# Two heads at a time on the two halves of the matrix array, in a two-block transformer kernel

## The reference, cut to what matters

```python
def _stick_breaking(qc, kc, vc):          # 16 heads of 64
    z = einsum('bqhd,bkhd->bhqk', qblk, k) * scale
    strict = kpos[None, :] < qp[:, None]
    log_stay = where(strict, log_sigmoid(-z), 0.0)
    after = cumsum(log_stay, axis=3, reverse=True) - log_stay
    a = where(strict, exp(log_sigmoid(z) + after), 0.0)
    return einsum('bhqk,bkhd->bqhd', a, v)

def _ssd(x, dt, a_neg, bm, cm):           # 16 heads of 64, 2 groups of B and C
    ...
```

## Time and profile before

| | us |
|---|---|
| median of 3 runs | 2288.71 |
| the runs | 2276.47 to 2288.92 |
| span of the profiled execution | 2284.1 |
| PE busy | 2143.6 |
| DVE busy | 1436.7 |
| ACT busy | 1127.0 |
| POOL busy | 140.9 |

### The profile page before, as it was taken

How to read it: one execution, slowest core, us unless ns; L and a number is a source line. 1 busy time by engine, 2 the same in 40 slices (tenths; PEclk the granted TensorE clock), 3 DMA queues, 4 the chain that set the end, 5 groups by cost and what they waited for, 6 DMA issues and landing times.

```text
span 2284.1 us, 38164 instructions
## 1 busy us (share of the span) xinstructions
PE 2143.6 (94%) x14507; PEld 1938.2 (85%) x14507; DVE 1436.7 (63%) x2106; ACT 1127.0 (49%) x1783; POOL 140.9 (6%) x157
## 2 busy tenths in 40 slices
PE   6999899999979999999979979997999999997997
PEld 5788799799868899888979959986989988897995
DVE  6766688465566676566665555556667656666555
ACT  4576466344335586355434433344458635543432
POOL 1200000000010003100010010001000310001002
PEclk9999999999989999999989989998999999998998
DMA  6433455544635344333535544563534333353562
GB/s 220 158 119 125 145 184 184 185 151 163 225 135 190 120 143 132 129 111 112 178 118 184 203 148 148 173 219 129 184 124 136 130 130 111 111 185 112 184 206 88
DMA packets 271155, 350.25 MB, mean 153 GB/s; under 512 B 9915, under 2 KB 225693, under 8 KB 271005
## 3 DMA queue, kind: packets, MB, share of 16 engines
q1 hardware_dynamic: 270733, 347.19, 45.3%
q0 software_dynamic: 272, 1.05, 0.1%
HBM read 347.17 MB, written 1.05 MB: 152 GB/s over the span
## 4 chain that ended last, share of the span: by engine, by line
issue 84%; PE 9%; POOL 4%; DVE 2%; ACT 0%; DMA 0%; SPq 0%; POOLq 0%; DVEq 0%; ACTq 0%
PE ps L650 3%; PE ps L652 2%; PE ps L651 2%; POOL act_s L2186 2%; POOL x L2174 1%; POOL x L2176 1%; DVE ring_r L1531 0%; DMA ring<-in_w_in 0%; PE ps L792 0%; PE ps L820 0%; PE ps L805 0%; POOL small L2151 0%; PE ps L757 0%; DVE act_s L1805 0%; DVE xT_r L1531 0%
## 5 line engine op out<-in xcount | busy, mean ns | idle before, releaser
L1531 DVE TENSOR_TENSOR ring_r<-ring,ring_hi 128x1024 fp32r<-128x1024 f32 x642 | 780.3, 1224 | 539.9 <-ACT ring_hi L1108 536.9
L1108 ACT ACTIVATE ring_hi<-ring 128x1024 fp32r<-128x1024 f32 x642 | 674.9, 1058 | 792.4 <-PE ps L652 737.8
L650 PE MATMUL ps<-xT_hi,ring_hi 128*128 128x256 f32 x2912 | 835.2, 287 | 36.9 <-DVE xT_r L1531 20.3
L651 PE MATMUL ps<-xT_r,ring_hi 128*128 128x256 f32 x2912 | 823.2, 283 | 0.0
L652 PE MATMUL ps<-xT_hi,ring_r 128*128 128x256 f32 x2912 | 823.0, 283 | 0.0
L650 PEld LDWEIGHTS ps<-xT_hi,ring_hi 128*128 128x128 f32 x2912 | 555.6, 191 | 52.3 <-issue 29.9
L651 PEld LDWEIGHTS ps<-xT_r,ring_hi 128*128 128x128 f32 x2912 | 555.6, 191 | 0.1
L652 PEld LDWEIGHTS ps<-xT_hi,ring_r 128*128 128x128 f32 x2912 | 555.1, 191 | 0.0
L652 PE MATMUL ps<-ring_hi,tok_r 128*128 128x512 f32 x536 | 212.6, 397 | 0.0
L650 PE MATMUL ps<-ring_hi,xT_hi 128*128 128x512 f32 x432 | 178.5, 413 | 15.3 <-DVE xT_r L1531 11.5
L651 PE MATMUL ps<-ring_r,xT_hi 128*128 128x512 f32 x432 | 174.2, 403 | 0.0
(11 more groups left out here) (280 smaller groups left out, 2616.7 us busy)
## 6 DMA issues: line engine op xcount, KB each, us to landing
ring<-in_w_mix_in SPq DMA_DIRECT2D x92, 1024.0 KB, 4.9
ring<-in_ffn_w_in SPq DMA_DIRECT2D x88, 1024.0 KB, 5.0
ring<-in_ffn_w_out SPq DMA_DIRECT2D x44, 1024.0 KB, 4.9
ring<-in_w_branch SPq DMA_DIRECT2D x24, 1024.0 KB, 5.3
ring<-in_w_in SPq DMA_DIRECT2D x22, 1024.0 KB, 5.0
ring<-in_w_ffn_up SPq DMA_DIRECT2D x22, 1024.0 KB, 5.0
ring<-in_w_ffn_down SPq DMA_DIRECT2D x11, 1024.0 KB, 5.0
ring<-in_w_mix_out SPq DMA_DIRECT2D x8, 1024.0 KB, 5.0
```

Source lines behind the costliest of these rows:

```text
L650: pe.matmul(out_, stat[0], mov[0], start=first, stop=False)
L651: pe.matmul(out_, stat[0], mov[1], start=False, stop=False)
L1108: act.activation(half_of(ring_hi[:, s % HIGHS, :], s, q), half_of(ring[:, s % SLOTS, :], s, q), ACT.Copy).then_inc(w_hi, 1)
L1531: return dve.tensor_tensor(lo, whole, hi.bitcast(F32), ALU.subtract)
```

## The change

Heads go in pairs p. In the plan the state-space stage keeps 18 beats, of which every second is empty; the stick-breaking stage has 22 beats, in turn (`osplit` p-3, `kout` p-2, `kscore` p) and (`ksum` p-1, `ksoft` p). `kscore` issues both heads' scores together, on the two row halves into S0 and S1; `sout` and `kout` issue both heads' values together, on the two column halves of one bank. `sdecay` and `ksum` issue the same matmuls as before, two heads in a row. `ksum` writes S0 and S1 in place of TB. Four buffers take the place of two: state-space matrices lie in `ex` and `lmat` (DVE multiplies in place), stick-breaking scores in `sm` and `wt`, softplus in `soft4`, which covers `lmat` and `cbm`. The waits follow. ACT, DVE and POOL do per pair what they did per head; not shown are the parts of their steps that only change the numbering. The core of the diff:

```diff
-    beats += beats_of(NH, ("sout", "sdecay"), (2, 0))
+    for p in range(NH // 2 + 1):
+        beats += [([("sout", p - 1)] if p else []) + ([("sdecay", p)] if p < NH // 2 else []), []]
     beats += [[("ysquare", 0)], [("snorm", 0), ("ysquare", 1)], [("snorm", 1)]]
-    tail = beats_of(NH, ("osplit", "kout", "ksum", "ksoft", "kscore"), (4, 3, 2, 1, 0))
+    tail = [beat for pairs in zip(beats_of(NH // 2, ("osplit", "kout", "kscore"), (3, 2, 0)),
+                                  beats_of(NH // 2, ("ksum", "ksoft"), (1, 0)) + [[], []]) for beat in pairs]
     tail[1].append(("bsplit", 0))
     tail[1].append(("bsplit", 1))
...
+        soft4 = tok[:, 0:4 * CAUS].rearrange("p (a n) -> p a n", a=4)
+
+        def decay_of(u):
+
+            return (ex if u % 4 < 2 else lmat)[:, u % 2, 0:CAUS]
+
+        def stick_of(u):
+
+            return (sm if u % 4 < 2 else wt)[:, u % 2, 0:CAUS]
...
-                def causal_pair(out_bank, lhs0, lhs1, rhs):
-
-                    pe.matmul(ps[:, out_bank, 0:TOK], lhs0, rhs[:, 0:TOK], start=True, stop=True)
-                    return pe.matmul(ps[:, out_bank, TOK:CAUS], lhs1, rhs[:, P:TOK], start=True, stop=True)
-
-                def causal_values(m, b, v0, v1, w):
-
-                    r = slice(HD * m, HD * (m + 1))
-                    pe.matmul(ps[r, b, 0:TOK], v0, w[:, 0:TOK], start=True, stop=False)
-                    return pe.matmul(ps[r, b, P:TOK], v1, w[:, TOK:CAUS], start=False, stop=True)
+                def causal_pair(out_banks, lhs0, lhs1, rhs):
+
+                    for b, w, m in zip(out_banks, lhs0, rhs):
+                        pe.matmul(ps[:, b, 0:TOK], w, m[:, 0:TOK], start=True, stop=True)
+                    for b, w, m in zip(out_banks, lhs1, rhs):
+                        mm = pe.matmul(ps[:, b, TOK:CAUS], w, m[:, P:TOK], start=True, stop=True)
+                    return mm
+
+                def causal_values(b, p, v, w):
+
+                    for t in range(T):
+                        for m in range(2):
+                            u = 2 * p + m
+                            o = ps[HD * m:HD * (m + 1), b, t * P:TOK]
+                            mm = pe.matmul(o, v[:, t, u * HD:(u + 1) * HD], w[m][:, 0:TOK] if t == 0 else w[m][:, TOK:CAUS],
+                                           start=(t == 0), stop=(t == 1))
+                    return mm
...
-                def sdecay(u):
-                    b = S0 + u % 2
-                    pe.wait_ge(seg_built, lap(L, u + 1, NH))
...
+                def sdecay(p):
+                    pe.wait_ge(seg_built, lap(L, 2 * p + 2, NH))
...
+                        pe.wait_ge(seg_exp, lap(L, 2 * p, NH))
+                    for m in range(2):
+                        b = S0 + m
+                        w = seg_w[:, m, :]
...
+                        pe.matmul(ps[:, b, 0:TOK], w[:, 0:P], upto, start=True, stop=False)
+                        pe.matmul(ps[:, b, P:TOK], w[:, 2 * P:3 * P], upto[:, 0:P], start=False, stop=True)
+                        pe.matmul(ps[:, b, TOK:CAUS], w[:, P:2 * P], upto[:, 0:P], start=True, stop=True).then_inc(seg_ready, 1)
...
+                def sout(p):
+                    pe.wait_ge(l_ready, lap(L, 2 * p + 2, NH))
...
+                    if p >= 2:
                         pe.wait_ge(y_gated, lap(L, p - 1, NH // 2))
+                    causal_values(TB + p % 2, p, xs, [decay_of(2 * p + m) for m in range(2)]).then_inc(y_ready, 1)
...
-                        pe.wait_ge(s_masked, lap(L, u - 1, NH))
-                    causal_pair(S0 + u % 2, kcT[r, pair, 0:P], kcT[r, pair, P:TOK], qcT[r, pair, :]).then_inc(s_score, 1)
+                        pe.wait_ge(s_masked, lap(L, 2 * p, NH))
+                    if p >= 2:
+                        pe.wait_ge(s_arg, lap(L, 2 * p - 2, NH))
+                    r = [slice(HD * m, HD * (m + 1)) for m in range(2)]
+                    causal_pair([S0, S1], [kcT[m, p, 0:P] for m in r], [kcT[m, p, P:TOK] for m in r], [qcT[m, p, :] for m in r])\
+                        .then_inc(s_score, 1)
+
+                def ksum(p):
+                    for u in (2 * p, 2 * p + 1):
+                        pe.wait_ge(s_soft, lap(L, u + 1, NH))
+                        b = S0 + u % 2
+                        if u % 2 == 0:
+                            pe.wait_ge(s_masked, lap(L, min(2 * p + 4, NH), NH))
+                        sp_ = soft4[:, u % 4, :]
+                        pe.matmul(ps[:, b, TOK:CAUS], from_on, sp_[:, TOK:CAUS], start=True, stop=True)
+                        pe.matmul(ps[:, b, 0:TOK], from_on, sp_[:, 0:TOK], start=True, stop=False)
+                        pe.matmul(ps[:, b, P:TOK], ones, sp_[:, TOK:CAUS], start=False, stop=True).then_inc(s_sum, 1)
...
+                def kout(p):
+                    pe.wait_ge(s_exp, lap(L, 2 * p + 2, NH))
...
+                    if p:
+                        pe.wait_ge(s_copied, lap(L, p, NH // 2))
...
+                    causal_values(OB, p, vc, [ex[:, m, 0:CAUS] for m in range(2)]).then_inc(s_out, 1)
...
+                def sdecay(p):
+                    for u in (2 * p, 2 * p + 1):
+                        act.wait_ge(seg_ready, lap(L, u + 1, NH))
+                        if u < 2:
+                            act.wait_ge(d_turned, lap(L, 2 * DH, 2 * DH))
+                        elif u >= 4 and u % 2 == 0:
+                            act.wait_ge(y_ready, lap(L, p - 1, NH // 2))
+                        act.activation(decay_of(u), ps[:, S0 + u % 2, 0:CAUS], ACT.Exp).then_inc(seg_exp, 1)
...
+                def kscore(p):
+                    for u in (2 * p, 2 * p + 1):
+                        b = soft4[:, u % 4, :]
+                        act.wait_ge(s_abs, lap(L, u + 1, NH))
+                        chain.link(act.activation(b, b, ACT.Exp, scale=-1.0))
                     chain.sync()
-                    act.activation(b, b, ACT.Ln, bias=1.0).then_inc(s_log, 1)
...
+                def ksum(p):
+                    for u in (2 * p, 2 * p + 1):
+                        act.wait_ge(s_arg, lap(L, u + 1, NH))
+                        if u % 2 == 0:
+                            if p == 0:
+                                act.wait_ge(y_ready, lap(L, NH // 2, NH // 2))
+                            else:
+                                act.wait_ge(s_out, lap(L, p, NH // 2))
+                        act.activation(ex[:, u % 2, 0:CAUS], stick_of(u), ACT.Exp).then_inc(s_exp, 1)
...
+                def sdecay(p):
...
+                    for u in (2 * p, 2 * p + 1):
+                        dve.wait_ge(seg_exp, lap(L, u + 1, NH))
+                        g = u // (NH // 2)
+                        e = decay_of(u)
+                        for t, r in enumerate((slice(0, TOK), slice(TOK, CAUS))):
+                            ins_ = dve.scalar_tensor_tensor(e[:, r], e[:, r], dts[:, 2, t * NH + u:t * NH + u + 1],
+                                                            cbm[:, g, r], ALU.mult, ALU.mult)
+                        ins_.then_inc(l_ready, 1)
...
+                def kscore(p):
...
+                    dve.wait_ge(s_score, lap(L, p + 1, NH // 2))
+                    if p >= 2:
+
+                        dve.wait_ge(s_exp, lap(L, 2 * p - 2, NH))
+                        dve.wait_ge(s_sum, lap(L, 2 * p - 2, NH))
+                    for u in (2 * p, 2 * p + 1):
+                        dve.scalar_tensor_tensor(stick_of(u), ps[:, S0 + u % 2, 0:CAUS], SCALE, cst("strict_neg"), ALU.mult, ALU.add).then_inc(s_masked, 1)
+                    for u in (2 * p, 2 * p + 1):
+                        z = stick_of(u)
+                        dve.wait_ge(s_masked, lap(L, u + 1, NH))
+                        dve.scalar_tensor_tensor(soft4[:, u % 4, :], z, -1.0, z, ALU.mult, ALU.max).then_inc(s_abs, 1)
...
+                def ksum(p):
+                    for u in (2 * p, 2 * p + 1):
+                        z = stick_of(u)
+                        dve.wait_ge(s_sum, lap(L, u + 1, NH))
+                        dve.tensor_tensor(z, z, ps[:, S0 + u % 2, 0:CAUS], ALU.subtract).then_inc(s_arg, 1)
...
+                    for u in (2 * p, 2 * p + 1):
+                        if p:
+                            pool.wait_ge(seg_ready, lap(L, u - 1, NH))
+                        for n, (m, t) in enumerate(((after, 0), (after, 1), (ones, 1))):
+                            ins_ = pool.tensor_tensor(seg_w[:, u % 2, n * P:(n + 1) * P], m,
+                                                      dts[:, 4, t * NH + u:t * NH + u + 1].to_broadcast([P, P]), ALU.mult)
+                        ins_.then_inc(seg_built, 1)
 
```

More of the change, by code:

```diff
@@ L274, in mixer_steps @@
     for n in range(2):
-        before(("drain", qc[n], 0), ("kscore", NH // 2 * n))
-        before(("drain", kc[n], 0), ("kscore", NH // 2 * n))
-        before(("drain", vc[n], 0), ("kout", NH // 2 * n))
+        before(("drain", qc[n], 0), ("kscore", NH // 4 * n))
+        before(("drain", kc[n], 0), ("kscore", NH // 4 * n))
```

(38 more changed lines are left out.)

130 lines of the change are left out of this document (29 added, 101 removed).

## The result

The changed kernel takes 2233.8 us (median of 4 runs, 2232.2 to 2235.7) against 2287.8 us (4 runs, 2276.5 to 2288.9; these are the three runs given above and one more): ratio 0.9775, 95% interval 0.9752 to 0.9799 (the two medians alone give 0.9764). The span of its profiled execution is 2233.9 us, 50.2 us shorter than before, and the one execution that is profiled took 2235.7, so only 1.8 us lie around its span.

The account below looks back on a forecast made before the run. PE's own work was taken to bound both head stages. Span 2284.1 us, less 49.0 saved, plus 1.0 of waits, gives 2236.1; 4.6 more around the span makes 2241 us, range 2227 to 2262.

Parts of the forecast that it names:

- What bounds: In both head stages PE's executed work sets the end; DVE would rise to 74% and ACT to 66%, still under PE.
- The overlap of halves: In kscore, sout and kout the second head is free: a pair takes one head's 0.85, 0.80 and 0.80 us.
- the rival with the column halves in sequence: Heads in sout and kout run one after the other: 20.5 us go back, 2261 us; chance 0.04.
- The rule quoted from the Trainium skill: Weight loads overlap matmuls in flight only where row groups differ; read as making sout's and kout's heads run in sequence.
- ksum keeps its matmuls: 8 x (0.90 + 0.87): sdecay and ksum each cost 0.90 us for the first head and 0.87 for the second; 28.3 us per layer for both.
- an entry and exit of 0.17 each: Every visit between big projection halves pays 0.17 us; 27 visits after the change, 4.6 us per layer.
- the visits of before: Small head operations and 37 entries and exits in the kernel before, put at 77.0 us per layer.
- New waits: Added PE waits in ksum, kscore and kout, taken as 0.5 us a layer, 1 us in all.
- Chain (c): kout waits for both heads' Exp, behind the subtractions after ksum; margin about 1.7 us, less what ACT has queued.
- chain (a): ksum waits until the following pair's scores are masked, since it writes the score banks; margin about 1.7 us.
- Rivals 1, 3 and 4: 1: halves don't overlap, 2272 us, 0.05. 3: late DVE masks, slower, 2304 us, 0.02. 4: no change, 2289 us, 0.02.
- Rival 2: Halves overlap, but shorter beats make PE wait in ksum and kout: 19 us back, 2260 us; chance 0.10.

Follow-up runs that it names:

- same_half: head_first with every second head's values in sout and kout put on the same 64 array columns as the first head's; 2253.0 us.
- apart: Changed kernel with the same beats and buffers, but heads alternate by kind within a visit (sout, sdecay, sout, sdecay; kout, kscore, kout, kscore); 2267.7 us.
- sout_by_four: Changed kernel with sout of two pairs in one visit, every fourth beat; visits 50.8 against 52.3 us, stage 1.5 us shorter per layer; total time not given.
- bsplit_apart: Changed kernel with the second bsplit moved two beats later; 2228.1 us against 2232.1 for the changed kernel in the same set.
- changed_again: The changed kernel itself, repeated as the reference of a later set; 2232.1 us, ratio 0.9763 to the kernel before.
- late_masks: Changed kernel with DVE's 1.22 us weight split left ahead of kscore's masks; 2243.8 us.
- head_first: Changed kernel issuing all products of one head before those of the other, for scores and values; 2234.7 us.

## Why the prediction was right, point by point

It forecast 2241 (2227 to 2262); measured 2233.8.

- What bounds: right. The whole saving lies in PE's work in the two stages (51.0 us by visits, 50.8 by the stages, 50.2 by span), DVE and ACT went to 73% and 65% (forecast 74% and 66%) and stayed covered.
- The overlap of halves: right, steps of 0.80 and 0.86 us for two heads (groups of eight records, of which the prediction speaks as four). same_half shows the price without it (20.6 us by the visits; forecast 20.5) and thereby the rival with the column halves in sequence. The rule quoted from the Trainium skill speaks of weight loads, and the trace does not agree with it for these column halves: the eight loads of sout (892.86 to 893.49) run while its matmuls do. The prediction made more of the rule than it says, serial products; in same_half, where the products do follow one another, loads run beside matmuls as well.
- "ksum keeps its matmuls: 8 x (0.90 + 0.87)" plus an entry and exit of 0.17 each: mis-sized. I took 0.90 from sdecay behind sout, where it pays for a part of the change of shape, and added an entry and an exit on top. ksum alone costs 1.75 for two heads, which is 2 x 0.87 and nothing more, not 1.94; eight of them, and a first sdecay of 1.82, make 1.6 us a layer, 3.3 us in all. Against that, I had put the visits of before 0.6 us a layer too high. It is the largest error among the terms, and it hid a gain: ksum in a visit of its own, with full-array work on both sides, needs no change of shape at all.
- The price of a change of shape, which the prediction spread over entries, exits and steps, can be read as one number. The products of a visit take 0.64 us for a head or an overlapping pair of sout, kout or kscore (same_half: 10.3 us for 16 second heads) and 0.87 for a head of sdecay or ksum. What a visit takes beyond that, divided by the number of changes between full array, column halves and row halves in it:

  | visit | us | its products | changes | each |
  |---|---|---|---|---|
  | sout alone | 1.00 | 0.64 | 2 | 0.18 |
  | kscore alone | 1.05 | 0.64 | 2 | 0.20 |
  | sout, two sdecay | 2.75 | 2.39 | 2 | 0.18 |
  | kout, kscore | 1.85 | 1.28 | 3 | 0.19 |
  | before: kout, ksum, kscore | 2.90 | 2.15 | 4 | 0.19 |
  | apart: sout, sdecay, sout, sdecay | 3.73 | 3.03 | 4 | 0.18 |
  | apart: kout, kscore, kout, kscore | 3.47 | 2.56 | 5 | 0.18 |
  | ksum alone, two heads | 1.75 | 1.75 | 0 | |

  The kernel before has 96 such changes in a layer and the changed one 42. So the 25.5 us a layer are 24 x 0.64 = 15.4 of overlap, about 54 x 0.18 = 9.7 of changes of shape, and 0.4 of waits. This division is an estimate from these rows; same_half shows the first part for sout and kout, and apart and sout_by_four agree with the second.
- New waits, "0.5 us a layer": the sign was wrong. Chain (c), which gave 1.4 us before, gives nothing now; chain (a) gives 1.1 us at the first ksum, where I had written that the bsplits "stayed where they were" and counted them at nothing. They are the cause (bsplit_apart). The margin of about 1.7 us of chain (a) was right (masks end at 998.0 at the latest, ksum starts at 999.83). The net is 0.4 us less per layer instead of 0.5 more: 1.8 us.
- The sum: the terms saved 48.0 us in the forecast, 51.0 by the visits and 50.2 by the span. Of the 7.2 us by which 2241 lies too high, 2.2 are the span (2236.1 against 2233.9), 0.3 rounding, 1.9 that the profiled execution lies above its median, and 2.8 the step from span to time: I added 4.6 us around the span, taken from a median that need not belong to the profiled execution, and after the change it is 1.8. That step weighed as much as all terms together. And these parts are finer than the profiles repeat: the same kernel has a span of 2233.9 us here and 2230.5 in changed_again. That the forecast span came within 2.2 us is partly luck; that the two stages were forecast 24 us shorter a layer and got 25.4 shorter is not.
- Rivals 1, 3 and 4 are out. Rival 2 did not happen here, but late_masks shows that it is near: 2 us of delay on DVE give back 12 us by the stage, 8 to 12 by the times.

## What to carry to other kernels

Where an engine's work is the bound, look for small products that leave half the array unused: here two on different rows or columns cost what one costs, and a row of the same kernel that already issues them so is worth more than a rule. Price small operations by the gap they open between the big ones around them, with the same neighbours: in this kernel each change of array shape costs 0.18 to 0.20 us, so an operation of another shape between big ones costs about 0.37 us beyond its products, and grouping equal shapes saves it. Here that was two fifths of the gain. And before relying on a margin, read the queue of the engine that must deliver at its most crowded beat, not at the usual one.

## What the runs showed of the hardware that I had not expected

A wait of PE of 3.14 us was followed by matmuls at the half rate (0.21 us apart instead of 0.12; granted clock 0.71 and 0.86 in the next two stretches of 4 us) and cost about 1.8 us more than it lasted, 1.6 of them by the clock, in both layers alike (9.20 and 9.19 us from this ksum to the next visit); a wait of 2.2 us in the same place left the clock at 1.00 (7.62 us). Eight records issued one head after the other overlap just as those issued in turn (head_first, a step of 0.80 us). And a full-array group between full-array matmuls costs nothing beyond its columns (ksum, 1.75 us for two heads), so a visit as such has no price; the change of shape has.
